# Gate and up products of three FFNs as Strassen blocks

## What is computed

```python
def modulate(h, shift, scale):
    return h * (1 + scale) + shift

def swiglu(h, w_gate, w_up, w_down):
    return (jax.nn.silu(h @ w_gate) * (h @ w_up)) @ w_down
...
        m_lat = jnp.split((silu_c @ ada_w[l] + ada_b[l])[:, None, :], N_MOD, axis=-1)
        m_ctx = jnp.split(silu_cc @ ada_w[l] + ada_b[l], N_MOD, axis=-1)

        def half_ffn(t, m, j):
            h = modulate(rmsnorm_2(t, norm_g[l, j]), m[3 * j], m[3 * j + 1])
            return t + 0.5 * m[3 * j + 2] * swiglu(h, ffn_w_gate[l, j // 2], ffn_w_up[l, j // 2],
                                                  ffn_w_down[l, j // 2])

        x = half_ffn(x, m_lat, 0)
        if ctx_read:
            ctx = half_ffn(ctx, m_ctx, 0)
```

## Time and profile before

| | us |
|---|---|
| three runs | 2232.43, 2233.87, 2236.87 |
| median | 2233.87 |
| span of the profiled execution | 2228.6 |
| PE busy in it | 2192.8 (98%) |
| POOL busy | 1340.7 (60%) |
| DVE busy | 1034.6 (46%) |
| ACT busy | 838.6 (38%) |

### The profile page before, as it was taken

How to read it: one execution, slowest core, us unless ns; L and a number is a source line. 1 busy time by engine, 2 the same in 40 slices (tenths; PEclk the granted TensorE clock), 3 DMA queues, 4 the chain that set the end, 5 groups by cost and what they waited for, 6 DMA issues and landing times.

```text
span 2228.6 us, 38801 instructions
## 1 busy us (share of the span) xinstructions
PE 2192.8 (98%) x13476; PEld 1955.2 (88%) x13484; DVE 1034.6 (46%) x2062; ACT 838.6 (38%) x1296; POOL 1340.7 (60%) x704
## 2 busy tenths in 40 slices
PE   8899999999999999999999999999999999999998
PEld 8899999999888888878888888888888988999998
DVE  7643377544755551377555324655522520233223
ACT  5455554555522222324222223322222422665444
POOL 6765887759655554424555444555544644458997
PEclk9999999999999999999999999999999999999999
DMA  8943479534555543413555333555433422325555
GB/s 301 275 154 105 152 260 281 185 105 152 186 192 192 197 129 93 126 42 142 193 197 197 122 96 109 198 197 197 175 86 105 168 95 95 104 86 187 187 180 154
DMA packets 112404, 356.41 MB, mean 160 GB/s; under 512 B 13224, under 2 KB 21928, under 8 KB 111920
## 3 DMA queue, kind: packets, MB, share of 16 engines
q1 hardware_dynamic: 112304, 355.07, 48.1%
HBM read 347.40 MB, written 1.05 MB: 156 GB/s over the span
## 4 chain that ended last, share of the span: by engine, by line
PE 83%; POOL 5%; issue 4%; DVE 4%; DMA 1%; ACT 1%; SPq 0%; POOLq 0%; DVEq 0%; ACTq 0%
PE ps L2111 23%; PE ps L2113 23%; PE ps L2112 23%; POOL w_low L1176 5%; PE ps L2160 2%; PE ps L2162 2%; PE ps L2161 1%; PE ps L2282 1%; PE ps L2617 1%; DMA raw<-in_wv_dram 1%; PE ps L2250 1%; DVE ps L1421 1%; PE ps L2316 1%; DVE h_low L1427 1%; PE ps L2511 1%
## 5 line engine op out<-in xcount | busy, mean ns | idle before, releaser
L1176 POOL TENSOR_TENSOR w_low<-raw,w_high 128x1024 fp32r<-128x1024 f32 (+3 forms) x542 | 1200.2, 2224 | 630.4 <-ACT w_high L637 629.5
L637 ACT ACTIVATE w_high<-raw 128x1024 fp32r<-128x1024 f32 (+3 forms) x544 | 536.8, 989 | 1072.0 <-PE ps L2113 847.9
L2111 PE MATMUL ps<-h_high,w_high 128*128 128x256 f32 (+2 forms) x2408 | 800.3, 332 | 6.7 <-POOL w_low L1176 6.0
L2112 PE MATMUL ps<-h_low,w_high 128*128 128x256 f32 (+2 forms) x2408 | 790.7, 328 | 0.0
L2113 PE MATMUL ps<-h_high,w_low 128*128 128x256 f32 (+2 forms) x2408 | 790.6, 328 | 0.0
L2111 PEld LDWEIGHTS ps<-h_high,w_high 128*128 128x128 f32 x2408 | 452.6, 188 | 52.9 <-issue 5.9
L2113 PEld LDWEIGHTS ps<-h_high,w_low 128*128 128x128 f32 x2408 | 453.2, 188 | 42.6
L2112 PEld LDWEIGHTS ps<-h_low,w_high 128*128 128x128 f32 x2408 | 453.3, 188 | 42.3
L2111 PE MATMUL ps<-act_high,w_high 128*128 128x256 f32 (+1 forms) x1058 | 345.6, 327 | 1.5 <-DVE act_low L2047 1.5
L2112 PE MATMUL ps<-act_low,w_high 128*128 128x256 f32 (+1 forms) x1058 | 344.7, 326 | 0.0
L2113 PE MATMUL ps<-act_high,w_low 128*128 128x256 f32 (+1 forms) x1058 | 344.7, 326 | 0.0
(11 more groups left out here) (251 smaller groups left out, 2203.1 us busy)
## 6 DMA issues: line engine op xcount, KB each, us to landing
raw<-in_w_dram SPq DMA_DIRECT2D x216, 512.0 KB, 3.3
raw<-in_wu_dram SPq DMA_DIRECT2D x176, 512.0 KB, 4.3
ada<-in_ada_dram SPq DMA_DIRECT2D x144, 512.0 KB, 3.6
raw<-in_wd_dram SPq DMA_DIRECT2D x64, 384.0 KB, 3.1
raw<-in_wd_dram SPq DMA_DIRECT2D x64, 320.0 KB, 2.9
raw<-in_wv_dram SPq DMA_DIRECT2D x24, 408.0 KB, 5.4
heads<-rot SPq DMA_DIRECT2D x96, 64.0 KB, 4.8
ada<-in_cond_dram SPq DMA_DIRECT2D x6, 512.0 KB, 5.0
```

The costliest lines, as they stand in the source:

```text
L637: e.activation(wh[:, c % RING, at_:at_ + w], raw[:, c % RING, 0:w], ACT.Copy).then_inc(hi_done, 1)
L1176: e.tensor_tensor(wl[:, c % RING, at_:at_ + w], raw[:, c % RING, 0:w], wh[:, c % RING, at_:at_ + w].bitcast(F32), ALU.subtract).then_inc(l ...
L2111: e.matmul(ps[:, bank, to:to + n], wh[:, j, w], hi, start=(first and t == tiles[0]), stop=False)
L2112: e.matmul(ps[:, bank, to:to + n], wh[:, j, w], low, start=False, stop=False)
```

## The change

Of the 22 pairs of each `up{f}`, f = 0, 1, 2, the first two stay as they were (`CLASSIC`). The other 20 (`NS`) are done as 2 x 2 blocks by Strassen's scheme in Winograd's form. The weights of a pair are the block matrix [gate; up] by two halves of the sum index (four k tiles each): A11, A12 (gate), A21, A22 (up). The moving operand is split into the halves of the sum index by latents and context: B11, B21 (latents), B12, B22 (context). Seven block products replace eight; each is 4 k tiles x 3 matmuls of 256 columns, so a pair is 84 matmuls of 256 columns where it was 48 of 512.

The sums that this needs:

- POOL makes four weight sums S1 to S4 (128 x 512 each) and the low parts of A11 and A12.
- ACT makes the high parts of A11 and A12; it copies S1 to S4 and A22 to PSUM and makes their high parts; it copies three partial results from PSUM to SBUF (keep P1, U2, U4), and does two silus of 256 columns.
- DVE makes five low parts from the PSUM copies, three additions of results, and two products silu x up, of 256 columns each.
- Once for each FFN the sums T1 to T4 of the moving operand are made in PSUM, by ACT and DVE in turn, in two parts. For this the norm also keeps a plain fp32 copy of its 16 tiles (`plain_h`, one more ACT operation each).

What else moves: the products of the rows with the context vector leave `up{f}` and stand in `down{f}`, where the rows are loaded again, 40, 40 and 8 of them (`CTX_ROWS`), some before each output's addition (`CTX_AT`). In `up{f}` stay 40 rows with one product each. The finishing of the rows moves from the end of `up{f}` to the seventh output of `down{f}` (and in down1 one row's to the first), and ACT's wait for it to the splits of the last output. The hidden activations are kept in fp32 (`act`) and split behind the pairs: 22 high parts by ACT, 4 low parts by POOL, 18 by DVE.

The diff, cut to its core (PE first, then DVE, SP and ACT):

```diff
+                def iteration(n, par):
+                    p2(n)
+                    p6(n, par)
+                    p7(n)
+                    p5(n, par)
+                    p1(n + 1, 1 - par)
+                    p3(n, par)
+                    p4(n)
...
+                def p6(n, par):
+                    e.wait_ge(t_split, 8 * f + 7)
+                    e.wait_ge(lo_sum, c0 + 5 * n + 1)
+                    e.wait_ge(p1_kept, p0 + n + 1)
+                    half(w_bank(par), AT_S2, (th[2], tl[2]), 0, 0, False).then_inc(st_done, 1)
...
+                for t in range(ACT_BY_POOL, FT):
+                    e.wait_ge(tile_high, FT * f + t + 1)
+                    e.tensor_tensor(al[:, t, :], act[:, t, :], ah[:, act_high_at(t), :].bitcast(F32), ALU.subtract)\
+                        .then_inc(tile_low_d, 1)
...
+                for o in range(KT - 1):
+                    for _ in range(CTX_AT[f][o]):
+                        modulate2(op0 + k, k % 2, (op0 + k) // 2, LAT_ROWS * f + k, 1, ada_down)
+                        k += 1
+                    if o in (0, KT - 2):
+                        e.wait_ge(ada2_done, 2 + op0 + k)
+                        for l_row in own_rows if o else first_rows:
+                            finish_row(*l_row)
+                    add_tile(f, lj, o, o % 2, 2)
...
+                for o in range(KT - 1):
+                    for _ in range(CTX_AT[f][o]):
+                        ada2_row(f, k, op0 + LAT_ROWS + k, ada_down)
+                        k += 1
+                    if o + 2 < KT:
                         for j in range(RING):
...
+                            e.wait_ge(lo_done, d0 + RING * (o + 2) + j + 1)
+                            down_load(o + 2, j)
...
                 before_high, behind_high, rest = steps
+                e.wait_ge(mod_ready, (9, 14, 19)[f])
```

More of the change, by code:

```diff
@@ L735, in turned_by_act, with half_norms @@
                 e.activation(pq[:, b, tt, g, :], ps[:, n % 4, 0:BINS], ACT.Copy).then_inc(f1_by_act, 1)
-            def half_norms(l, jn, dest, done, nxt, widths, second=range(KT), between=lambda k: None):
+            def half_norms(l, jn, dest, done, nxt, widths, second=range(KT), between=lambda k: None, keep_plain=False):
                 shift = mod_shift(l, 3 * jn)
@@ new lines, in up @@
+                sum_high(0, 0, 4)
+                classic(1)
+                a22(0, 0)
+                e.wait_ge(cond_in, 16 * LAYERS + 32 * f + 16)
+                e.wait_ge(t_split, 8 * f + 8)
+                e.activation(cond_bank(0), ada_up[0][:, :], ACT.Silu).then_inc(c_silu, 1)
+                e.wait_ge(st_done, base + 1)
+                keep_p1(0)
+                a11(1, 1)
+                with e.Fori(0, NS // 2 - 1) as i:
+                    for par in range(2):
+                        iteration(2 * i + par, par, True)
@@ L1790, in down @@
                 return tail
-            up(0, 2, [(0, row) for row in range(3, 8)])
+            up(0)
             e.wait_ge(own_std, 1)
@@ L1800, in _ @@
             own(KT)
-            tail = down(0, 0)
+            tail = down(0, 0, [(0, row) for row in range(3, 8)])
             def turned_by_dve(n):
@@ L1916, in _ @@
             n_nsplit(2 * KT)
-            up(1, 2, [(0, 8)] + [(1, row) for row in range(4)])
-            tail = down(1, 2)
+            up(1)
+            tail = down(1, 2, [(1, row) for row in range(4)], [(0, 8)])
             root(SUM_BANK[0])
@@ L1924, in _ @@
             n_nsplit(2 * KT)
-            up(2, 2, [(1, row) for row in range(4, 9)])
-            tail = down(2, 3)
+            up(2)
+            tail = down(2, 3, [(1, row) for row in range(4, 9)])
             root(SUM_BANK[0])
@@ new lines, in half @@
+                def half(bank, s, move, k0, lo, first):
+                    mh, ml = move
+                    out = ps[:, bank, 0:T]
+                    for t in range(KT // 2):
+                        at_ = LINE + HALF * (s % 2) + P * t
+                        high, low = wh[:, s // 2, at_:at_ + P], wl[:, s // 2, at_:at_ + P]
+                        hi, lo_ = mh[:, k0 + t, lo:lo + T], ml[:, k0 + t, lo:lo + T]
+                        e.matmul(out, high, hi, start=(first and t == 0), stop=False, skip_group_check=not first)
+                        e.matmul(out, high, lo_, start=False, stop=False, skip_group_check=not first)
+                        end = e.matmul(out, low, hi, start=False, stop=(t == KT // 2 - 1), skip_group_check=not first)
+                    return end
```

617 lines of the change are left out of this document (507 added, 110 removed).

## The result

The changed kernel takes 2296.84 us (median of 4 runs, 2282.57 to 2304.67), the kernel before 2235.24 (median of 4, 2232.43 to 2236.87). The ratio is 1.0268, 95% interval 1.0231 to 1.0304: slower by 2.7%, 62 us. The profiled execution is the fastest of the four (2282.57, span 2280.8, which is 52.2 above that of before). The forecast was 2254, with a range up to 2285: the right sign, a third of the size.

What follows compares the result with a forecast made beforehand. PE was taken to bound the kernel, busy 98%. The terms -71 + 26 + 15 + 40 + 7 + 3 = +20 gave some 2249 us on the span, 2254 on the median; range 2205 to 2285.

Steps and rivals of the forecast that it cites:

- PE's stream: In the up loops, a pair falls from 10.88 to 9.70 us on PE; 60 pairs, -71 us (-83 to -58).
- The start of each up: PE waits for ACT's copy of P1, 8.0 us in up1 and up2, 10.4 in up0: +26 us (20 to 32).
- The end of each up: Down's first matmuls wait for the last silu, products and DVE's low parts, 5.2 us each: +15 us (5 to 22).
- The rows in down0 and down1: Rows through two buffers end late and delay the last split; PE waits, +23 and +17, sum +40 us (5 to 60).
- The 10 for additions and squares: In down0 and down1, six additions with squares hold DVE 3.5 us each, about half under a landing: 10 us.
- the forecast's own next steps: After down's rows: finish 5.3 us, ACT's split 0.7, POOL 1.6, handovers 0.25; PE wants the last k tiles at 114.
- The clock: After waits of 8 us or more PE runs slow steps, 1.4 us lost each, five such waits: +7 us (0 to 11).
- The norm's copies: In the norm, 48 plain ACT copies of 0.38 us, mostly hidden; +1 per FFN, +3 us (1 to 8).
- The rows keep pace: Rival: rows of down0 and down1 end before PE needs the last chunk; 2199 to 2222 us, chance 0.25.

Runs made afterwards that it cites:

- the runs above: Changed kernel with four buffers for the rows of down (2211.19 us), and that version with product P2 done three times more at each up's start (2215.14 us).
- the first combined version: Changed kernel with four buffers for down's rows, ACT's wait for finished rows at the next norm's first tile, and P1's copy earlier: 2218.49 us, ratio 0.9932.

## Why the prediction was wrong, step by step

- **PE's stream (-71).** Right. In up0 and up2 the step is 0.1133, a pair 9.52 us, in up1 it is 0.1178, a pair 9.90: 27.3 + 27.3 + 19.7 = 74 saved. Every engine kept up: PE was busy 20.00 of 20 us in the loop's stretches.
- **The start of each up (+26).** Right in place, a little too dear: the waits on ACT's copy of P1 are 9.1, 5.0 and 6.4 us, 20.4 in all. Moving the copy alone gains little, since the alternation of ACT and DVE behind it makes PE wait at the next products.
- **The end of each up (+15).** Right in place: PE waits 8.9 us on DVE's low parts, and 0.9 for the first k tile. Without any rows the three downs are 5.9, 6.0 and 4.5 us longer than before, 16 in all.
- **The rows in down0 and down1 (+40).** The mechanism was right, down to the late split behind ACT's wait (forecast 15 and 9 us, measured 9.7 and 5.5, after more had been lost on the way). The term was mis-sized: without the rows the two stages are 71 us shorter. The step that failed is "A row lands in 3.6 us median in the FFN, some 3.4 when fewer loads fly", with the 95 us for 40 rows made of it. In down0 the mean landing was 4.8, at 232 GB/s, where the row of before was from a stretch at 192 GB/s. That the bytes on the way lengthen a landing, the runs show from several sides: 2.9 us for half a row, 5.8 and 6.0 with three and four rows on the way, 3.9 for the rows with no weight load beside them and 5.3 for the others, and 4.4 once the loads are spread. Why even the rows with no load beside them take 3.9 and not 3.4 is open; another row is mostly on the way then. The chain took 122 us instead of 95 + 10 = 105. The 10 for additions and squares was wrong as well, to the other side: nearly all of it lies under the longer landings, and leaving the squares out gave 4 us a stage. With 122 and 123 us for the rows and the start of the rows as measured (26.0 and 19.3 us), the forecast's own next steps (5.3 for the finish, 2.55 for the last split, PE ready at 114) give +42 and +36 for its +23 and +17; the two stages lost 45 and 38. So this one step makes up the 32 us by which the forecast missed the profiled span, and a little more.
- **The clock (+7).** The mechanism was right, the count was not: of "Five of the new waits are 8 us or more" two came so, 9.1 and 9.7. But shorter waits drew the lower clock as well (in the runs above it was 0.50 behind waits of 4.2 and of 5.6 us), at 16 places, 26 us of PE's time. Some 14 of these lie in down0 and down1 ahead of PE's last wait for the rows. By the trace they cost nothing of their own there: DVE never waits for PE between the first row and the last, so a faster PE would only have waited longer for the last split. That leaves some 12 against the forecast's 7.
- **The norm's copies (+3).** Three stretches with a norm are 2.5, 4.1 and 3.3 longer, 10 in all, about 3 of it slow steps, the rest not traced further.
- **The sum.** -74 for the stream, +20 and +5 for the starts and the slow steps behind them, +16 for the ends, +71 for the rows and +10 for the stretches with a norm are 48 of the span's 52; the rest was not traced. The median missed by 10 us more than the span, since the profiled execution was the fastest of the four; the step of 256 columns in the other executions (last section) may be the cause, but they have no trace.
- **Rivals.** "The rows keep pace" gave 1.95 us per row as the point from which it decides, with the additions counted apart, which is 2.2 with them, and 2199 to 2222 as its time. With four buffers a row takes 86 / 40 = 2.15 with its additions, and the time is 2211: that rival described the kernel that the change could have been. Its argument against itself (each row is issued only when its buffer is free) is what held.
- **The range.** The term of the rows was bounded at 60 us; they cost 71 in the two stages.

## What to carry to other kernels

When work is moved to a stage with room on an engine, price its transfers by what will be in flight in that stage, not by their landing where they come from: landing, product and reissue in turn, over the number of buffers, is the pace as long as the landings set it (with two buffers 123 us by the formula and 122 measured; with four 73 and 86, so the rest of DVE's work shows), and here two more buffers of 512 KB turned 2.7% slower into 0.9% faster. Use the mean landing, not the median, where bursts of other loads pass between the transfers. A new wait of some microseconds of a busy PE costs more than itself where no later wait for the same chain follows, since here the matmuls behind waits of 2.9 to 9.7 us ran at half the clock for a while and lost 1.0 to 2.7 us.

## What the hardware showed that I had not expected

A matmul of 256 columns had two steps here, and kept one of them for a whole stage. Three stretches of 20 us of the changed kernel, in up0, up1 and up2, with PE busy throughout and the granted clock at 1.00:

```profile
620.00:640.00 20.00, 20.00 (x179) 20.00 (x178) 15.27 (x30) 17.63 (x38) 15.88 (x13) 1.00 0.65 231
1095.00:1115.00 20.00, 20.00 (x172) 20.00 (x171) 14.86 (x29) 16.96 (x36) 15.54 (x13) 1.00 0.61 215
1490.00:1510.00 20.00, 20.00 (x179) 20.00 (x178) 15.28 (x30) 17.64 (x38) 15.54 (x13) 1.00 0.62 223
```

179, 172 and 179 matmuls: 0.1133 and 0.1178 us. Of the 36 ups in the traces of the changed kernel and the 11 experiments nine had the longer step, and the same stage with the same instructions had now the one and now the other (up1 took 207.2 us in the kernel with the rows left out and 200.2 in the one with four buffers, which differ in down alone). It also shows in the last FFN, which no kernel changed: 482 to 485 us from the last down to the end with the short step, 489 and 490 with the long. Over 20 pairs it is 7.5 us, so that three ups and the last FFN can make an execution some 30 us longer or shorter; the seven of the first combined version span 25 us, and those of the kernel before beside them, which has 256-column matmuls in other stages, 14. That the spread comes from the step is not shown, since one execution of each kernel was traced. What chooses the step stays open; no run here was made for it. Comparisons of a few microseconds between kernels with many 256-column matmuls are therefore better read stretch by stretch than from the medians.

POOL and DVE hold each other up in both directions. The same eight scalings of DVE (line 2227 and its like) took 4.6 and 4.9 us in the two traces where two of POOL's splits ran in that time, and 8.4 to 8.8 us in the others, with four. In the run with the copy of P1 earlier, one of POOL's splits took 7.27 us while DVE's low parts ran on beside it at their usual 0.68 each; the same split took 1.90 in the changed kernel.
